# The router of a two-layer MoE decoder fed from the state ahead of its norm, and value weights split later

## What is computed

```python
for i in range(2):
    mix = swa_sink_attention(...) if i == 0 else forgetting_attention(...)
    x = layer_norm(ALPHA * x + mix, ln_gain[i, 0], ln_bias[i, 0])
    # grouped_moe:
    logits = x @ w_router + b_router            # [512, 16]
    scores = softmax(logits)                    # best group of 4 experts by its top 2, then its 2 experts
    y = sum over the 2 experts of gate * (silu(x @ w_gate) * (x @ w_up)) @ w_down
    x = layer_norm(ALPHA * x + y, ln_gain[i, 1], ln_bias[i, 1])
```

## Time and profile before

| what | us |
|---|---|
| median of the three runs | 920.74 |
| the profiled execution | 919.96 |
| its span, first to last instruction | 918.2 |
| PE busy | 888.0 (97%) |
| DVE busy | 552.9 (60%) |
| ACT busy | 392.3 (43%) |
| POOL busy | 120.1 (13%) |

### The profile page before, as it was taken

The page is one execution under the profiler, slowest core; times in us unless marked ns, Lnnn a source line. Parts: engine busy times, 40 slices in busy tenths (PEclk is TensorE's granted clock), DMA queues, the critical chain, the costliest instruction groups (busy, mean ns, idle before and its releaser), DMA issues.

```text
span 918.2 us, 12501 instructions
## 1 busy us (share of the span) xinstructions
PE 888.0 (97%) x4480; PEld 616.2 (67%) x4480; DVE 552.9 (60%) x1141; ACT 392.3 (43%) x787; POOL 120.1 (13%) x138
## 2 busy tenths in 40 slices
PE   8999999999999999989999999999999999999996
PEld 7887777884666665557878886655786565666553
DVE  4544786548766677773332223777456777677846
ACT  4322787001555655540132224777301355555540
POOL 2000232103010000120000000323111200000030
PEclk9999999999999999999999999999999999999999
DMA  9962000019999998644054222120106999999352
GB/s 347 302 253 92 2 1 1 24 47 351 350 382 389 379 389 322 222 180 163 21 184 138 92 93 92 46 71 24 69 24 241 312 380 382 374 384 406 124 197 96
DMA packets 49446, 182.36 MB, mean 199 GB/s; under 512 B 6496, under 2 KB 6496, under 8 KB 41200
## 3 DMA queue, kind: packets, MB, share of 16 engines
q1 hardware_dynamic: 35712, 132.34, 38.6%
q0 software_dynamic: 9392, 34.12, 11.3%
q10 hardware_dynamic: 4288, 15.21, 4.2%
HBM read 159.60 MB, written 22.05 MB: 198 GB/s over the span
## 4 chain that ended last, share of the span: by engine, by line
PE 89%; DVE 5%; DMA 3%; issue 2%; ACT 1%; SPq 1%; POOL 0%; DVEq 0%; ACTq 0%; POOLq 0%
PE bank L613 17%; PE bank L615 16%; PE bank L614 16%; PE bank L896 11%; PE bank L727 4%; PE bank L708 4%; PE bank L865 3%; PE bank L570 3%; PE bank L752 2%; PE bank L771 2%; PE bank L527 2%; DMA ring<-in_swa_w_in 2%; PE bank L813 2%; PE bank L541 1%; DMA ys<-arena 1%
## 5 line engine op out<-in xcount | busy, mean ns | idle before, releaser
L1492 DVE TENSOR_TENSOR gu_low<-ring,gu_high 128x1024 fp32r<-128x1024 f32 x128 | 151.2, 1221 | 46.9 <-ACT gu_high L1116 46.8
L1116 ACT CAST gu_high<-ring 128x1024 fp32r<-128x1024 f32 x128 | 127.6, 1048 | 18.5 <-DVE arena L1626 18.5
L896 PE MATMUL bank<-ring,arena 128*96 128x512 f32 x256 | 115.8, 595 | 2.0 <-issue 2.0
L613 PE MATMUL bank<-gu_high,rows_high 128*96 128x512 f32 x256 | 113.0, 442 | 2.5 <-DVE rows_low L1610 2.5
L614 PE MATMUL bank<-gu_low,rows_high 128*96 128x512 f32 x256 | 101.5, 397 | 0.0
L615 PE MATMUL bank<-gu_high,rows_low 128*96 128x512 f32 x256 | 101.1, 395 | 0.0
L896 PEld LDWEIGHTS bank<-ring,arena 128*96 128x96 f32 x256 | 39.7, 164 | 55.0 <-issue 54.0
L1048 ACT ACTIVATE arena<-arena,nmax 128x256 f32<-128x256 f32 (+3 forms) x128 | 66.8, 523 | 20.9 <-DVE nmax L1385 10.8
L471 POOL TENSOR_TENSOR low<-ring,high 128x512 fp32r<-128x512 f32 x32 | 40.7, 1272 | 220.5 <-ACT high L1076 220.5
L613 PE MATMUL bank<-high,x_high 128*128 128x512 f32 x160 | 64.2, 401 | 1.3 <-DVE low L1286 1.1
L615 PE MATMUL bank<-high,xlow 128*128 128x512 f32 x160 | 62.9, 393 | 0.0
(11 more groups left out here) (244 smaller groups left out, 1543.7 us busy)
## 6 DMA issues: line engine op xcount, KB each, us to landing
ring<-in_w_gate SPq DMA_DIRECT2D x32, 1024.0 KB, 12.3
ring<-in_w_up SPq DMA_DIRECT2D x32, 1024.0 KB, 15.0
ring<-in_w_down SPq DMA_DIRECT2D x32, 1024.0 KB, 14.9
ring<-in_fox_w_in SPq DMA_DIRECT2D x6, 2048.0 KB, 9.4
ys<-arena ACTq DMA_DIRECT2D x28, 384.0 KB, 7.7
ys<-lnp POOLq DMA_DIRECT2D x1, 4608.0 KB, 24.3
ring<-in_swa_w_in SPq DMA_DIRECT2D x2, 2048.0 KB, 17.2
ring<-in_swa_w_o SPq DMA_DIRECT2D x2, 2048.0 KB, 15.9
```

The costliest lines, as they stand in the source:

```text
L613: eng.matmul(out, ah, wh, start=(c == 0), stop=False)
L896: mm = eng.matmul(bank[5 + half][0:CAP, :], hT[:, b, c, :], w[:, c, half * BLK:(half + 1) * BLK], start=(c == 0), stop=(c == FC - 1))
L1116: eng.copy(gu_high[u % 2][:, :, part, :], slot_gate_up(use)[:, :, part, :]).then_inc(S("gu_high"), 1)
L1492: eng.tensor_tensor(gu_low[use % RING][:, :, part, :], slot_gate_up(use)[:, :, part, :], gu_high[u % 2][:, :, part, :], ALU.subtract).then ...
```

## The change

The router's weights are prepared once on the chip for both layers, so that the logits can be made from the state ahead of its norm. With v the state, m and r its mean and 1/deviation, g and c the norm's gain and bias, and W the router's weights, `((v - m) r g + c) W = r (v (gW - column mean of gW)) + cW`. During the input projection of layer 0, PE turns 32 rows of gains and biases and sums the weighted columns with a matrix of ones (8 matmuls of 64 columns); DVE makes the products and the differences.

`turn_x` of the states ahead of the router then waits for the residual (`res_done`) and not for the norm. DVE copies the turned tile first and norms it after (`turned_norm`), since the norm overwrites the tile. The fillers ahead of the turn of tile 3 go from 16 to 4. DVE multiplies the logits by rstd, one more operation. ACT copies a turned tile ahead of its wait for `x_ready` and the store. Two quarters of the first expert's low weights stand behind tile 1 and two behind tile 2.

DVE's eight splits of the second value block become two ahead of the statistics of tile 0 and six behind the low part of tile 0. Two semaphores are merged into others: the rotation table's into `x_in1` (the turn of tile 1 at the start now waits for both), and the turned gates' into `opened`, with the opening of the banks put ahead of the turn.

```diff
-                        ... cs ... .then_inc(S("rope_in"), 16)
+                        ... cs ... .then_inc(S("x_in1"), 16)
-                        eng.dma_start(wr[:, :, :], w_router...)
+                        eng.dma_start(wr_in, w_router...)
+                        for i in range(2 * DEPTH):
+                            vec = (ln_gain, ln_bias)[i % 2][i // 2, 0]
+                            eng.dma_start(ln_rows[KC * i:KC * i + KC, :], vec.rearrange("(c p) -> c p", p=P)).then_inc(S("const_in"), 16)
@@ PE
             def turn_x(t, a):
                 if a == "in":
-                    eng.wait_ge(S(f"x_in{t}"), 16)
+                    eng.wait_ge(S(f"x_in{t}"), 32 if t == 1 else 16)
+                elif a in ("00", "10"):
+                    eng.wait_ge(S("res_done"), 2 * (t + 1) + OUT_BLOCKS * NT * int(a[0]))
                 else:
                     eng.wait_ge(S(f"x_ready{a}"), t + 1)
...
+                            if k == GROUPS[0] - 4:
+                                eng.wait_ge(S("const_in"), 144)
+                                eng.transpose(bank[7][:, 0:4 * KC], ln_rows[0:4 * KC, :], ident[0:4 * KC, 0:4 * KC]).then_inc(S("wr_pe"), 1)
+                            if k == GROUPS[0] - 3:
+                                eng.wait_ge(S("consts"), 1)
+                                eng.wait_ge(S("wr_dve"), 1)
+                                for c in range(KC):
+                                    mm = eng.matmul(bank[7][:, 0:4 * NE], ones, wr_ln[:, c, :, :]..., ...)
+                                mm.then_inc(S("wr_pe"), 1)
+                    eng.wait_ge(S("wr_dve"), 2)
...
-                hum(16)
+                hum(4)
                 turn_x(NT - 1, f"{l}0")
...
+                open_banks(l, 0)
                 for h in range(2):
                     for t in range(NT):
                         mm = eng.transpose(bank[h]..., hot_in[t]..., ident[:, :])
-                mm.then_inc(S("hot_turned"), 1)
-                open_banks(l, 0)
+                mm.then_inc(S("opened"), 1)
@@ ACT
                 for t in range(NT):
+                    evac_x(f"{l}0", t)
                     eng.wait_ge(S(f"x_ready{l}0"), t + 1)
                     eng.dma_start(xd[t * P:(t + 1) * P, :], xres[:, t, :]).then_inc(S("x_stored"), 16)
-                    evac_x(f"{l}0", t)
@@ DVE
+                        if k == GROUPS[0] - 3:
+                            eng.wait_ge(S("wr_pe"), 1)
+                            link(eng.tensor_copy(ln_cols, bank[7][:, 0:4 * KC]))
+                            for i in range(2 * DEPTH):
+                                ins = eng.tensor_tensor(wr_ln[:, :, i, :], wr_in, ln_cols..., ALU.mult)
+                            ins.then_inc(S("wr_dve"), 1)
                         if k == GROUPS[0] - 1:
+                            eng.wait_ge(S("wr_pe"), 2)
+                            for m in range(DEPTH):   # per layer: 1/D scale, subtract, add of b_router
+                                ...
...
+                def turned_norm(t):
+                    v = xres[:, t, :]
+                    evac_x_tile(f"{l}0", t)
...
+                    link(eng.scalar_tensor_tensor(v, v, mv[:, t, 0:1], lnp[:, 0, :], ALU.subtract, ALU.mult))
+                    eng.wait_ge(S(f"rstd{l}0"), t + 1)
+                    eng.scalar_tensor_tensor(v, v, rstd[:, t:t + 1], lnp[:, 1, :], ALU.mult, ALU.add).then_inc(S(f"x_ready{l}0"), 1)
                 for t in range(NT):
                     for b in range(OUT_BLOCKS):
                         (residual, res_done)
-                        if t >= 1 and b == 0:
-                            evac_x_tile(f"{l}0", t - 1)
                         link(half_stats(t, b))
-                    norm(l, 0, t)
-                    if t >= 1:
-                        gate_up_low(0, 0, t - 1, t)
-                evac_x_tile(f"{l}0", NT - 1)
-                gate_up_low(0, 0, NT - 1, SPLITS)
+                        if t >= 1 and b == 0:
+                            turned_norm(t - 1)
+                    (bn_aggr, veps, ln_stats)
+                    if t in (1, 2):
+                        gate_up_low(0, 0, 2 * t - 2, 2 * t)
+                turned_norm(NT - 1)
...
-                link(eng.tensor_tensor(lg, lps, tiles(br[:, :]), ALU.add))
+                link(eng.tensor_tensor(lg, lps, over(rstd[:, :], NE), ALU.mult))
+                link(eng.tensor_tensor(lg, lg, tiles(bl[:, l, :]), ALU.add))
...
-                    value_weights_low(KC, 2 * KC)
+                    value_weights_low(KC, KC + 2)
...
                             if b == 0 and t >= 1:
                                 state_low(t - 1)
+                                if t == 1:
+                                    value_weights_low(KC + 2, 2 * KC)
```

More of the change, by code:

```diff
@@ L78, in trunk @@
         sink = sb("sink", [P, NH])
-        wr = sb("wr", [P, KC, NE])
+        wr = sb("wr", [P, DEPTH, KC, NE])
         wf = sb("wf", [P, KC, NH])
         br = sb("br", [P, NE])
+        bl = sb("bl", [P, DEPTH, NE])
         bf = sb("bf", [NH, 1])
@@ L116, in trunk @@
         ones, before = area(14352, P), area(14352 + P, P)
+        wr_in = area(12288, KC * NE, "p (c n) -> p c n", c=KC)
+        ln_rows, ln_cols = area(12416, P), area(12544, 4 * KC)
+        wr_ln = area(12608, KC * 4 * NE, "p (c j n) -> p c j n", c=KC, j=4)
         cb = lnp[:, :, :].rearrange("p b (h n) -> p b h n", h=2)
@@ L337, in _ @@
                         load_x(1)
[L338 removed]
+                        eng.dma_start(cs[:, :, :, :], rope.rearrange("(t p) a n -> p t a n", p=P)).then_inc(S("x_in1"), 16)
                         load_x(2)
@@ L549, in open_banks @@
                                     start=True, stop=True)
-                mm.then_inc(S("opened"), 1)
+                if t > 0:
+                    mm.then_inc(S("opened"), 1)
             def mix_all(l, t, more):
@@ L644, in _ @@
                                 turn_heads(k - 1)
+                            if k == GROUPS[0] - 4:
[5 more added lines that the diff above has]
+                                for c in range(KC):
+                                    mm = eng.matmul(bank[7][:, 0:4 * NE], ones, wr_ln[:, c, :, :].rearrange("p j n -> p (j n)"),
+                                                    start=(c == 0), stop=(c == KC - 1))
+                                mm.then_inc(S("wr_pe"), 1)
+                    eng.wait_ge(S("wr_dve"), 2)
                 else:
@@ L1194, in _ @@
                     step(NE // 4 - 2, u, last=(u == 7))
-                eng.wait_ge(S("hot_turned"), l + 1)
+                eng.wait_ge(S("opened"), 2 * l + 1)
                 for h in range(2):
@@ L1298, in _ @@
                 in_weights_low(p)
-            eng.wait_ge(S("rope_in"), 16)
+            eng.wait_ge(S("x_in1"), 32)
             for l in range(DEPTH):
@@ L1311, in _ @@
                         j, t = k // NT, k % NT
-                        if k == GROUPS[0] - 1:
-                            eng.wait_ge(S("const_in"), 80)
+                        if k == GROUPS[0] - 3:
+                            eng.wait_ge(S("wr_pe"), 1)
+                            link(eng.tensor_copy(ln_cols, bank[7][:, 0:4 * KC]))
+                            for i in range(2 * DEPTH):
+                                ins = eng.tensor_tensor(wr_ln[:, :, i, :], wr_in,
+                                                        ln_cols[:, KC * i:KC * i + KC].unsqueeze(2).to_broadcast([P, KC, NE]), ALU.mult)
+                            ins.then_inc(S("wr_dve"), 1)
+                        if k == GROUPS[0] - 1:
+                            eng.wait_ge(S("wr_pe"), 2)
+                            for m in range(DEPTH):
+                                col = 2 * m * NE
+                                link(eng.tensor_scalar(ln_cols[:, 0:NE], bank[7][:, col:col + NE], 1.0 / D, None, ALU.mult))
+                                link(eng.tensor_tensor(wr[:, m, :, :], wr_ln[:, :, 2 * m, :],
+                                                       ln_cols[:, 0:NE].unsqueeze(1).to_broadcast([P, KC, NE]), ALU.subtract))
+                                ins = eng.tensor_tensor(bl[:, m, :], bank[7][:, col + NE:col + 2 * NE], br[:, :], ALU.add)
+                            ins.then_inc(S("wr_dve"), 1)
+                            eng.wait_ge(S("const_in"), 144)
                             link(eng.tensor_scalar(sink[:, :], sink[:, :], -1.0, None, ALU.mult))
@@ L1493, in gate_up_low @@
                                           gu_high[u % 2][:, :, part, :], ALU.subtract).then_inc(S("gu_low"), 1)
+                def turned_norm(t):
+                    v = xres[:, t, :]
+                    evac_x_tile(f"{l}0", t)
+                    if t == 0:
+                        norms[0] += 1
+                        eng.wait_ge(S("ln_in"), 32 * norms[0])
+                    link(eng.scalar_tensor_tensor(v, v, mv[:, t, 0:1], lnp[:, 0, :], ALU.subtract, ALU.mult))
+                    eng.wait_ge(S(f"rstd{l}0"), t + 1)
```

(1 more changed line is left out.)

10 lines of the change are left out of this document (5 added, 5 removed).

## The result

The changed kernel took 923.89 us (median of 8 runs, 923.41 to 925.33), the kernel before 920.26 us beside it (919.72 to 922.89). The ratio is 1.0037, with a 95% interval of 1.0026 to 1.0048: slower by 3.4 us. The profiled execution of after took 924.33 us, with a span of 922.5 against 918.2, so its trace is 4.3 us longer from the first instruction to the last. Its mean granted clock was 0.988 against 0.996; in all eight runs it was 0.988 to 0.990.

A forecast was written before the change was run, and what follows sets the result against it. PE was taken to bound the kernel, carrying 89% of the chain. From 919.96: +1.05 +0.2 +0.3 -1.77 +0 (gates) +0.5 (clock) = 920.24; with 0.78 to the median, 921.0 us, range 915.8 to 924.0.

The forecast's parts named there:

- the likeliest case: Whole kernel: tile 3's store binds as reckoned at the gates, no measurable change, 919.0 to 923.0 us; chance 0.55.
- the slower rival: Gates: tile 3's store waits behind SP's queued packets, 1.6 us longer in each layer, 924.2 us; chance 0.13.
- preparation in the projection: Layer 0's input projection: 8 matmuls of 64 columns and a small turn on PE's path, +1.05 us (0 to 2.1).
- `row_ids` sooner at a gate: Router chain at each gate: turning ahead of the norm ends `row_ids` 2.02 us earlier.
- `x_ready` and store of tile 3 later: Gates: the copy goes ahead of the norm, so tile 3's `x_ready` and store come 1.79 us later.
- store leads, gather begins: Gates: POOL's first gather waits for tile 3's store, starting +0.3 us in layer 0 and -0.3 in layer 1.
- first turn of rows, both gates: Gates: the router's 2.02 us become 2.0 us of PE waiting for rows, so both gates together give 0.
- the clock: Gates: more PE idle makes a clock fall likely in layer 0; +0.5 us net, ends -1.7 and +1.7.
- boundary: Between the layers: moved splits let tile 0's turn start straight behind PE's work, -1.77 us (0 to -1.77).
- `residual(0)`: End of layer 1's experts: `residual(0)` comes two fillers later, +0.3 us (0 to 0.43); 0 in layer 0.
- the 1.2 us more that I had for it: Gates: if the skill's clock rule held, both gates would pay in full, making the sum 1.2 us higher.
- The first rival: Gates: stores land within 7.6 us and bind nothing, each gate gains 2.02 us, 916.5 us; chance 0.28.
- The third rival: Boundary: moving the splits gives nothing because another step of tile 0 comes last, 922.8 us; chance 0.04.

The follow-up runs named there:

- split_only: The kernel before with only DVE's splits of the second value block moved (two ahead of tile 0's statistics, six behind its low part); 917.92 us, ratio 0.9976.
- split_prep: The kernel before with the boundary's splits moved and the router weights' preparation made but unused, router and norm order unchanged; 921.04 us, ratio 1.0012.
- before_hold2: The kernel before with three of SP's five weight loads at each gate held until the first gather has landed; 932.71 us, ratio 1.0134.
- the three held forms of the changed kernel: The changed kernel, three SP loads per gate held until stores landed (929.07 us), until first gather landed (927.20), or the latter with POOL's norm loads behind its fourth gather (934.14).
- after_hold: The changed kernel with three of SP's five weight loads at each gate held until all four stores of the state have landed; 929.07 us, ratio 1.0098.

## Why the prediction came out as it did

It said 921.0, range 915.8 to 924.0, and the likeliest outcome no measurable change. The time was 923.9: in the range, outside the likeliest case's own (919.0 to 923.0), and slower by 0.37%, just above the 0.3% that it set. It was not the slower rival that came true: the store took 9.3 and 9.1 us, not 11.6. The mechanism forecast held, and two terms were too small. That the time is still inside the range is in part luck: the profiled execution was forecast at 920.24 and took 924.33, 4.1 us more. The medians are only 2.9 apart, since the profiled execution lay 0.44 above its median here and 0.78 below it in the kernel before.

| step of the sum | predicted | measured |
|---|---|---|
| preparation in the projection | +1.05 (0 to 2.1) | +2.02 in the traces of before and after, though after's start was 0.44 ahead; 2.7 by the mean mark of twelve traces |
| wait for the rotation table | +0.2 | 0 (turn of tile 1 at 12.12 for 12.56) |
| `row_ids` sooner at a gate | -2.02 | -2.01 and -1.45 |
| `x_ready` and store of tile 3 later | +1.79 | `x_ready` +1.80 |
| store leads, gather begins | +0.3 and -0.3 | -0.92 and -1.07 |
| first turn of rows, both gates | 0 | +0.43 and -0.05 |
| the clock | +0.5 (up to 1.7) | +1.4 at `wo`, 2.1 to 2.3 at gate 0, 0 at gate 1 against a fall of before's own |
| boundary | -1.77 | -1.60 (split_only: -1.76) |
| `residual(0)` | +0.3 | +0.33 |

**Preparation.** The step that failed is the reading of the earlier trace rows: "x8" was read as eight products, but it counts instructions, and there are four products of two each. Eight products are 16 records and 1.90 us, and 2.1 with the turn: the upper end of my range, by luck, since I had drawn that from another row. The code of that line would have told it: a call of `mix` with two blocks makes four products of the row's shape, and the row says 8. That is 1.1 us of the 4.1 missed in the profiled execution; the clock is 3.0.

**The clock.** I had the place and the reason (2 us more idle ahead of the rows in layer 0) and priced it at +0.5, because part of the fall lies in the wait. It didn't: the fall came with the wait's end and lasted to 238 us, through the first products. Against split_prep, whose gates had no fall, the fold lost 2.26 and 1.01 us, and with ten more fillers no gate had a fall and the third expert's turn came 2.32 and 1.18 us sooner. "TensorE: Matmul & The Clock Gate", section "HAM oscillation — how this bites in real kernels", of the Trainium skill says that a wait for a transfer ahead of a burst makes the burst start slow; its example waits longer, some 3 to 5 us. Here the trace agrees with it at both gates (2.37 and 1.42 us of wait), and the 1.2 us more that I had for it would have been the better term. It does not account for the fall at gate 1 of before, which had no such wait. The 1.4 us at the start of `wo` belong to no edit: split_only, split_prep and before_hold2 have that fall too, behind the same 0.84 us of idle that before and seven more of these kernels have without one.

**The gate.** The central claim held: the store takes the place of the router's chain. I had the gather starting level with before; it started 0.9 and 1.1 us sooner, because it follows the landing by 0.29 us and not by 0.8. What I left out took that back: the gather itself took 1.35 and 1.0 us longer (5.75 for 4.40, 5.58 for 4.56). No run shows why; the prediction had put POOL's two norm loads, which share its queue and now also go later, at 0, and no run moves them alone. The first rival needed the store to land within 7.6 us; it took over 9 in both layers. The rule on queues by which it would have ("DMA: Bandwidth & Descriptors", section "Queues, rings and completion order", of the Trainium skill) does not fit the store's time: beside SP's loads it took 9.1 to 10.5 us, so it did not go out in one turn. Nor was the prediction's share of one packet in three all of it, as the 3.5 us without any packet of the store show.

**The boundary** held to 0.17 us, and its own run to 0.01. The third rival is out.

What stays open: why the clock falls in one run and not in the next behind the same idle, why the gather takes longer with the fold, and 0.6 us of the preparation's 2.7 that are neither in the products nor in the turn.

## What to carry to other kernels

A chain that is shortened pays only down to the transfer beside it: before a step is moved ahead of a norm or a copy, look at what the normed value's own store and the gather behind it wait for, and at whether the transfer engines are full there. Where they are, as here, another order of requests can just move the wait to the next load (the three held forms of the changed kernel took 927 to 934 us). When PE is freed from a chain and waits for a transfer instead, count the clock's fall in full and let fillers last to the end of the new wait. And a single profile is not enough for a change of this size: 4 of 21 gates had a fall behind less than 0.4 us of idle, at some 1.5 us each.

## What the runs showed of the hardware

- A product of two plain fp32 operands shows as two instructions: 16 records, 1.90 us for eight of 64 columns (0.24 us each), 2 records and 0.33 us for one.
- A store of 0.5 MB took 9.1 to 10.5 us beside five loads of 1 MB, and 3.4 us with three of them held. Its first packet moved 3.5 us behind the issue in after and 0.7 in after_hold. A gather of 96 rows took 4.4 us at most beside emptied queues, 4.40 (before) to 5.75 us (after) beside the loads and 8.36 beside loads let go just ahead of it.
- The same kernel's runs differ by their clock: those of before in one batch went from 917.77 us at 0.997 to 921.90 at 0.992, about 0.8 us for each 0.001.
- Behind the same 0.84 us of idle at the start of `wo` the clock fell in four traces (after, split_only, split_prep, before_hold2) and not in eight (before and all others without fillers there).
- Seven gates had 0.72 to 4.57 us of idle ahead of their first turn of rows, all with a fall of the clock behind it; of the 21 with none to 0.53 us four had one.
